# Where the prompt tiles, their norms and the retention scores stand in the order of an eight-core decoder step

## The reference: what is computed

```python
for layer in range(2):
    h = rms_norm(x, norm_mix[layer])
    if layer == 0:                       # retention, 4 heads, dk 256, dv 512
        q, k = rotate(h @ w_q), rotate(h @ w_k) / 16
        v = h @ w_v
        # per chunk of 128 tokens, state s (256 x 512) per head:
        #   o = (q k^T * decay) v + decay * q s ;  s = decay * s + k^T v
        o = group_norm(o)
        x = x + (silu(h @ w_g) * o) @ w_o
    else:                                # attention over a window of 128, sinks
        x = x + attention(h) @ w_o + b_o
    h = rms_norm(x, norm_ffn[layer])
    x = x + (silu(h @ w1) * (h @ w3)) @ w2
y = rms_norm(x, norm_final)
```

## Time and profile before

| what | value |
|---|---|
| median of 3 runs | 1962.94 us (1962.29 to 1965.96) |
| the profiled execution: its time | 1966.23 us |
| its span, on the slowest core | 1965.2 us (cores 1955.5 to 1965.2) |
| PE busy | 1852.6 us (94%) |
| DVE busy | 875.5 us (45%) |
| ACT busy | 677.4 us (34%) |
| mean granted clock of PE, slowest core | 0.986 |

### The profile page before, as it was taken

How to read it: one execution, slowest core, us unless ns; L and a number is a source line. 1 busy time by engine, 2 the same in 40 slices (tenths; PEclk the granted TensorE clock), 3 DMA queues, 4 the chain that set the end, 5 groups by cost and what they waited for, 6 DMA issues and landing times.

```text
span 1965.2 us, 29635 instructions; the slowest of 8 cores (1955.5 to 1965.2 us)
## 1 busy us (share of the span) xinstructions
PE 1852.6 (94%) x10167; PEld 853.7 (43%) x10167; DVE 875.5 (45%) x1549; ACT 677.4 (34%) x1062; POOL 222.0 (11%) x363
## 2 busy tenths in 40 slices
PE   4999999999999999999979998999999998999997
PEld 1444444344444334443434444445454543445453
DVE  3565543434346663433655554332222555522225
ACT  3544432321224742223344444221012366410112
POOL 0111111010101001110011111111011110011010
PEclk9899999999999999999989999999999999999999
DMA  9435565898987349998746655665335330254352
GB/s 194 68 66 87 94 81 87 199 207 197 210 203 144 46 84 220 217 202 228 160 108 113 106 94 84 119 82 74 54 57 78 56 58 9 33 88 69 54 71 97
DMA packets 216449, 220.79 MB, mean 112 GB/s; under 512 B 47824, under 2 KB 171088, under 8 KB 216272
## 3 DMA queue, kind: packets, MB, share of 16 engines
q0 software_dynamic: 128112, 114.08, 41.3%
q1 hardware_dynamic: 88192, 104.83, 17.9%
HBM read 277.10 MB, written 48.89 MB: 166 GB/s over the span
## 4 chain that ended last, share of the span: by engine, by line
PE 81%; DVE 7%; DMA 4%; issue 3%; ACT 3%; DVEq 0%; POOL 0%; SPq 0%; ACTq 0%; POOLq 0%
PE ps L579 81%; DVE rt L603 2%; DMA x_62<-xTp 1%; DMA uT_64<-g_73 1%; ACT sq L595 1%; DMA wr<-wa 1%; DVE h_44 L606 1%; DVE stat L858 1%; DMA x_63<-xTp 1%; DVE x_62 L606 0%; DVE h_45 L606 0%; DVE x_62 L603 0%; PE ps L584 0%; DMA yTp<-x_62 0%; ACT L593 0%
## 5 line engine op out<-in xcount | busy, mean ns | idle before, releaser
L579 PE MATMUL ps<-h_44,wr 128*128 128x512 bf16 x1824 | 411.3, 381 | 14.1 <-DMA wr<-wa 8.6
L579 PE MATMUL ps<-h_45,wr 128*128 128x512 bf16 x1824 | 413.1, 380 | 0.0
L579 PEld LDWEIGHTS ps<-h_44,wr 128*128 128x128 bf16 x1824 | 174.5, 98 | 230.4 <-issue 31.7
L579 PEld LDWEIGHTS ps<-h_45,wr 128*128 128x128 bf16 x1824 | 173.9, 98 | 217.1 <-issue 18.2
L259 POOL DMA_DIRECT2D wr<-w x152 | 112.9, 745 | 1017.0 <-PE ps L579 914.3
L579 PE MATMUL ps<-aT_105,wr 128*128 128x512 bf16 x704 | 157.7, 379 | 1.6 <-DVE x_62 L603 1.6
L579 PE MATMUL ps<-aT_103,wr 128*128 128x512 bf16 x704 | 157.0, 379 | 1.4 <-DVE aT_136 L603 1.4
L595 ACT ACTIVATE s_104<-ps 128x512 f32<-128x512 f32 x88 | 52.5, 596 | 305.5 <-PE ps L579 284.2
L603 DVE TENSOR_TENSOR aT_105<-s_106,ps 128x512 bf16<-128x512 f32 x88 | 60.5, 688 | 208.0 <-PE ps L579 179.0
L603 DVE TENSOR_TENSOR aT_103<-s_104,ps 128x512 bf16<-128x512 f32 x88 | 60.5, 688 | 204.2 <-PE ps L579 184.9
L579 PE MATMUL ps<-wr,h_44 128*128 128x512 bf16 (+1 forms) x576 | 130.5, 375 | 6.2 <-ACT rstd_57 L595 3.6
(11 more groups left out here) (288 smaller groups left out, 2147.2 us busy)
## 6 DMA issues: line engine op xcount, KB each, us to landing
wr<-w POOLq DMA_DIRECT2D x88, 512.0 KB, 7.5
wr<-wa POOLq DMA_DIRECT2D x24, 1024.0 KB, 12.4
wr<-w POOLq DMA_DIRECT2D x64, 352.0 KB, 7.0
wr<-wo POOLq DMA_DIRECT2D x16, 512.0 KB, 8.9
S_0_107<-st_in SPq DMA_DIRECT2D x16, 512.0 KB, 6.2
S_1_108<-st_in SPq DMA_DIRECT2D x16, 512.0 KB, 6.6
S_2_109<-st_in SPq DMA_DIRECT2D x16, 512.0 KB, 7.7
S_3_110<-st_in SPq DMA_DIRECT2D x16, 512.0 KB, 6.6
```

The costliest lines, as they stand in the source:

```text
L579: self.S.op("pe", lambda e: e.matmul(out, lhsT, rhs, start=start, stop=stop, skip_group_check=skip), r, w, dur=k * max(0.1, self.n(out) * ...
```

## The change

Four edits.

1. **The fourth x tile.** T[0]'s final norm writes into tiles of its own (`yo0`, `yo4`, `yo7`), placed over memory that `ffn` no longer uses. When it is done, T[3] is loaded by four DMAs on SP, and then y is stored by three DMAs on ACT's queue. In `ret_layer` the load of the spilled states (`Sin`) comes first, in memory of its own; then `pre()` completes T[0]'s norm before the other tiles of the layer are placed.
2. **Scores.** In `Rp` the scores of chunks 0 and 1 are written before the output of chunk 0, and those of chunk c + 2 after the state update of chunk c.
3. **Banks.** The norm of the second tile after `w_o` takes bank 6 or 7.
4. **The start.** The loads of T[1] are written before unit 2 (g of head 0) and start when unit 0 has landed; unit 2 waits for the third quarter of T[1]; unit 3 waits for nothing of x.

```diff
@@ norm_do_out
-            o, ob = (cx.x, cx.xb) if j.to_x else (cx.h, cx.hb)
-            self.stt(o[:, kc, :NT], cx.x[:, kc, :NT], self.gain(j.gi, kc), j.rstd_ap[:, :NT], ALU.mult, ALU.mult,
-                     [cx.xb[kc], j.rstd_buf, self.spb], [ob[kc]])
+            if callable(j.dst):
+                j.dst = j.dst()
+            if j.dst:
+                out, outb = j.dst[kc]
+            else:
+                o, outs = (cx.x, cx.xb) if j.to_x else (cx.h, cx.hb)
+                out, outb = o[:, kc, :NT], outs[kc]
+            self.stt(out, cx.x[:, kc, :NT], self.gain(j.gi, kc), j.rstd_ap[:, :NT], ALU.mult, ALU.mult,
+                     [cx.xb[kc], j.rstd_buf, self.spb], [outb])
@@ ret_layer
-        Ar = Area(M, self.a0, self.rid0)
+        Ar = Area(M, self.rid0 - 8192, self.rid0)
+        Sin = [Ar.tile(f"Sin{i}", [128, 2, 512], F32) for i in range(2)]
...
+        load_sin(0)
+        load_sin(1)
+        pre()
+        Ar = Area(M, self.a0, self.rid0 - 8192)
@@ Rp
                 if c == 0:
                     pcs.append(sc_piece(n))
+                    pcs.append(sc_piece(n + 1))
                 pcs.append((3, lambda n=n: r_o(n), need_o(n)))
                 pcs.append((2, lambda n=n: r_su(n), need_su(n)))
-                if c < 3:
-                    pcs.append(sc_piece(n + 1))
+                if c < 2:
+                    pcs.append(sc_piece(n + 2))
@@ program
         def rest():
-            load_x(1, 4, [self.ring.cur[("v", 0)][2]], True)
+            load_x(1, 4, [self.ring.cur[("qk", 0)][2]], True)
             load_rope(1)
-        self.ring.start({0: T[0].xb[4:6], 3: T[1].xb}, {3: rest})
+        self.ring.start({0: T[0].xb[4:6], 2: T[1].xb[4:6]}, {2: rest})
...
-                           [lambda: self.norm_begin(ta, 1, NBK), lambda: self.norm_begin(tb, 1, NBK), lambda: self.norm_begin(scx, 1, NBK)], s == 1)
+                           [lambda: self.norm_begin(ta, 1, NBK), lambda: self.norm_begin(tb, 1, (6, 7)), lambda: self.norm_begin(scx, 1, NBK)], s == 1,
+                           lambda: self.norm_now(T[0]) if s == 1 else None)
...
                 def endA():
+                    ys = []
+                    def place():
+                        for k, n, off in ((0, 4, 0), (4, 3, 8192), (7, 1, HF * TT * 4 + 8 * TT * 4)):
+                            t_, tb_ = M.tile(f"yo{k}", [128, n, TT], F32, self.a0 + off, n)
+                            ys.append((k, n, t_, tb_))
+                        return [(t_[:, i, :], tb_[i]) for k, n, t_, tb_ in ys for i in range(n)]
                     def aft():
-                        store(0)
-                        load_x(3)
-                    return self.norm_begin(ta, 4, NBK, True, aft)
+                        load_x(3, 4)
+                        for k, n, t_, tb_ in ys:
+                            self.dma("act", yout[:, k:k + n, 0:TT], t_[:, :, :], tb_, [], f"yo{k}")
+                    j = self.norm_begin(ta, 4, NBK, True, aft)
+                    j.dst = place
+                    return j
```

More of the change, by code:

```diff
@@ L666, in norm_begin @@
         j.cx, j.gi, j.pool, j.to_x, j.after = cx, gi, pool, to_x, after
-        j.sq, j.mm, j.nmm, j.out, j.bk, j.half = [], [], 0, None, None, None
+        j.sq, j.mm, j.nmm, j.out, j.bk, j.half, j.dst = [], [], 0, None, None, None, None
         self.jobs.append(j)
@@ L885, in dq_tick, with ret_layer, load_sin @@
                 self.force(it)
-    def ret_layer(self, s, cxs, scx, idle, first_norms, norms, wo_rider):
+    def ret_layer(self, s, cxs, scx, idle, first_norms, norms, wo_rider, pre):
         M = self.M
-        Ar = Area(M, self.a0, self.rid0)
+        Ar = Area(M, self.rid0 - 8192, self.rid0)
+        Sin = [Ar.tile(f"Sin{i}", [128, 2, 512], F32) for i in range(2)]
+        def load_sin(h):
+            if s == 1 and h < RH:
+                self.dma("sp", Sin[h % 2][0][:, :, :], self.DR["spill"][h].rearrange("(a p) e -> p a e", p=128),
+                         [self.spillb[h]], Sin[h % 2][1], f"sin{h % 2}")
+        load_sin(0)
+        load_sin(1)
+        pre()
+        Ar = Area(M, self.a0, self.rid0 - 8192)
         uT0 = Ar.tile("uT0", [128, 16, TT], BF16, 16)
@@ L906, in ret_layer @@
         Sbf = [Ar.tile(f"Sbf{i}", [128, 2, 512], BF16) for i in range(2)]
-        Sin = [Ar.tile(f"Sin{i}", [128, 2, 512], F32) for i in range(2)]
         cf, cfb, cb, cbb = self.cf, self.cfb, self.cb, self.cbb
@@ L917, in ret_layer @@
                             g=Rr.tile(f"rg{h}", [128, 512], BF16))
[L919 to L924, removed]
         def P(h, ti, lead=False):
```

## The result

The changed kernel took 1950.88 us (median of 4 runs, 1949.41 to 1955.07), the kernel before 1964.45 us on the same chip (4 runs, 1962.29 to 1969.34): a ratio of 0.9931, 95% interval 0.9905 to 0.9957, 13.6 us faster. In a second comparison it took 1951.34 us, ratio 0.9923 (0.9905 to 0.9941). Forecast: 15.4 us faster, 1948.

A forecast was written before the change was run, and what follows sets the result against it. PE was taken as the bound, busy 1852.6 of 1965.2 us. Terms of -6.0, -9.5, -3.0 and +3.1 gave -15.4 us, from the median 1962.94 to 1947.5, stated as 1948; range 1938 to 1960.

The forecast's parts named there:

- The likeliest case: Whole kernel: 15.4 us faster, to 1948 us, with a range of 10 to 20 us faster; chance 0.47.
- 1, fourth tile: End of round 0: T[3] lands earlier through parallel loads, so the group at its norm starts sooner; 6.0 us gained.
- 2, scores: Retention outputs: masks written one chunk earlier remove PE's waits for `sT`; 9.5 us gained of 11.7 at most.
- 3, banks: Third group of `ffn` in each round: no more wait for the bank of the second tile's norm; 3.0 us gained.
- 4, start: Start: g lands later and PE stands for it, less a part regained by the clock; costs 3.1 us.
- a gain by the clock: Start: the group after the second g group runs at the high clock, 1.89 instead of 3.57 us; 1.7 us gained.
- a fifth was kept back: Score waits: four fifths of 11.7 us counted, 9.5, since the state's copy `Sbf` might end as late as the mask.
- The third rival: Score matmuls: PE stands for the first mask before the second score at all 16 pairs; 8.5 us slower, 1971; chance 0.08.
- the prediction's own +4.8: Start: the second g group begins at 55.7 instead of 50.92 us because g lands later; 4.8 us lost.
- The first rival: Start: g of head 0 lands at 43.3, before PE asks at 44.6; 22 us faster in all, 1941; chance 0.12.
- that I counted as none: Around T[3]'s norm: 2.7 us lost to low clock might return, but none was counted since 2 us of standing remain.
- the stand at the group that I feared for: PE's 0.84 us wait at 977.66 for T[1]'s norm, feared longer behind ACT's store issues; 1 us charged.

The follow-up runs named there:

- undo2: The changed kernel with the score reordering taken back; 1964.37 us, ratio 1.0002 to the kernel before.
- undo4: The changed kernel with the reordered start loads taken back; 1942.70 us, ratio 0.9900 to the kernel before; 1944.92 us, 0.9897 when repeated.
- only4: The kernel before with only the reordered start loads added; 1971.75 us, ratio 1.0028 to the kernel before.
- g_free: The changed kernel with T[1] still loaded early, but g of head 0 issued directly behind v, not held for T[1]; 1951.84 us, ratio 0.9921 to the kernel before.
- split: The changed kernel with only T[1]'s first two quarters loaded early, the last two after v, and g not held; 1946.29 us, ratio 0.9900 to the kernel before.
- undo1: The changed kernel with the fourth-tile change taken back: y in place, T[3] loaded by two serial halves; 1954.86 us, ratio 0.9951 to the kernel before.
- store_sp: The changed kernel with y's three stores on SP's queue behind the loads instead of on ACT's; 1953.34 us, ratio 0.9924 to the kernel before.
- undo3: The changed kernel with the use of banks 6 and 7 taken back; 1954.66 us, ratio 0.9956 to the kernel before.
- undo4_first67: The changed kernel without the reordered start loads, first norms of T[1] and T[3] also in banks 6 and 7; 1956.40 us, ratio 0.9946 to the kernel before.

## Why the prediction came out

The likeliest case held: faster by 13.6 us where 15.4 was said, inside the likeliest one's own range of 10 to 20. Term by term, each against its edit taken back (in us; the last four columns are means over cores, from one execution each; edit 4 also from its repeat):

| edit | predicted | by the ratios | mean span | standing | 0.16 x stands | clock |
|---|---|---|---|---|---|---|
| 1, fourth tile | -6.0 | -4 | -4.1 | -1.6 | +0.3 | -1.9 |
| 2, scores | -9.5 | -14 | -15.6 | -9.5 | -2.7 | -3.1 |
| 3, banks | -3.0 | -5 | -2.9 | -2.9 | -0.6 | +1.2 |
| 4, start | +3.1 | +6 | +5.4 | +5.3 | +0.2 | +1.1 |
| 4, repeated | +3.1 | +5 | +5.9 | +5.4 | +0.3 | +0.5 |

The four mean spans add up to -17.2, and the mean span fell by 17.7. The waits were found at the right places. What was off is their price: edit 2 was priced by the idle time of the listed waits alone, edit 1 on one core, and edit 4 with a gain by the clock that didn't come.

**Edit 2** is the term that was furthest off, and the mechanism held. All 11.7 us of `sT` went; 1.9 us for `Sbf` and some for `uT` came (a fifth was kept back for this). The third rival, a stand in front of the second score, didn't occur: no score matmul waits. From the first score matmul of a round to the first matmul of w2, both rounds together, undo2 takes 727.2 us and the changed kernel 713.3: 13.9 us, not 9.5. The list of waits leaves out gaps of 0.15 us and less: of the 64 matmuls on `sT`, 23 or 24 stand in undo2, 12.7 us in the mean over cores, not 13 with 11.7, and none in the changed kernel. Each stand costs 0.16 us on top, 3.8 us for these matmuls. The clock of the table needs care: 2.3 of its 3.1 us lie after 1300 us, behind the last matmul on `sT` (1220.8), and are not shown to be of this edit.

**Edit 4**. The mechanism held step by step: T[1]'s third quarter at 38.0 (36.7 predicted), g issued at 38.6 (37), landed at 50.5 (49.4), 11.9 us (12.4; 10.3 to 14.6 over the cores), second g group at 56.6 (55.7). From the first projection to the first score matmul the changed kernel takes 36.7 us in the mean over cores, undo4 31.9, and the repeats 37.5 and 32.7: 4.8 us both times, the prediction's own +4.8 without its clock. The step that failed is "the next group then runs at the high clock, 1.89 instead of 3.57 us: -1.7". Around the two stands the clock was low for 6.8 to 10.2 us on the eight cores, in the kernel before for 3.4 to 6.8 us, and on core 0 the second group ran at 3.45 us too. Part of this low time fell on standing, where it costs nothing; what PE lost while it worked was 0.8 and 1.2 us more at the start than without edit 4 (3.6 and 2.8; 3.8 and 2.6), and only4 lost as much as the kernel before (3.3 and 3.4). So nothing was given back. g_free and split show where the standing is from: part from holding g back until T[1] has landed (3.1 of 4.6 us of standing, 2.1 of 4.8 us of the stretch), the rest from T[1] sharing the DMA engines with v and g. The first rival, g in time, had no core for it: PE stood 3.8 to 8.2 us for g on all eight.

The Trainium skill, "DMA: Bandwidth & Descriptors", section "Anatomy of one DMA — SWDGE (gpsimd) path", gave an estimate of 6.8 us for g; the trace has 10.3 at the least, so the rows were the better guide.

**Edit 1**: the sum was right for the core it was read on. T[3] landed 15.2 us after its issue (986.68 - 971.47; 13 predicted) and the group at its norm came 9.8 us after PE was through with T[2]'s values (994.50 - 984.68; 9.3 predicted, 996.2 - 986.93). Of the wait of 4.42 us 2.49 remain, and the 11.9 us from the row sum to that group became 7.3 (994.50 - 987.17), as said, though not all by the cause that was said. PE's stand for the eviction of g, 1.53 us, is gone: ACT's squares run in one go, where those of the second half had come late and g behind them. But another 1.6 us are the clock: the first group of g took 3.51 us before and takes 1.89 now. And core 3 was the one whose tile came last. There the group came 16.3 us after T[2]'s values; on the other seven cores it was 13.1 to 14.6 before, and after it is 9.8 to 11.1 on all eight. The wait itself was 2.49 to 2.97 us on these seven already before, and after it is 2.49 or 2.50 on all eight. These 2.49 us are ACT's queue: its squares of T[3] begin at 985.25, behind the last `v` eviction, though the first quarter landed at 979.75.

From the end of T[2]'s values to T[3]'s first projection undo1 takes 19.4 us in the mean over cores and the changed kernel 14.7 (14.9 in its repeat): 4.7 us, of which 2.4 is standing (1.8 of it between the row sum and the group, 0.4 at the row sum) and most of the rest the clock, 0.97 or more in place of 0.90 to 0.93, that I counted as none. I charged 1 us for ACT's store issues; the stand at the group that I feared for is 0.86 us against 0.84, now for DVE's rotation, and store_sp shows that the queue doesn't matter.

The rule of the Trainium skill that transfers of all queues share the engines ("DMA: Bandwidth & Descriptors", "Issuing engines are not separate DMA queues") agrees: T[3] came in with y, 986.68 and 985.39. On this core it cost PE nothing, because ACT came to the squares no sooner.

**Edit 3**: 2.9 us of standing for 3.0, but the equality is luck. The two stands of 1.53 us are back in undo3 on all cores. Other waits before 1300 us are 2.2 us shorter there (those for `uT` 1.6), and after 1300 us it stands 2.0 us longer (1.9 of it for DVE's `aT`), where the prediction had nothing. Why was not tested.

That the sum was near is in part luck: edit 2 gave 4 us more than said, edit 4 cost 2 more and edit 1 gave 1 to 2 less.

## What to carry to other kernels

A load that is put ahead of another delays it twice, by the bytes in between and by the wait that orders them; compare when each is asked for first (T[1]'s squares here had to wait for ACT's `v` evictions anyway). Before pricing a wait at one core's number, read it on all cores: 4.42 us on the slowest, 2.49 to 2.97 on the others. Price a stand by when the next matmul starts, not by its idle time: here each cost 0.16 us more, and ten of 23 were too short for the list. Don't count on the clock to give something back behind a stand: here it gave nothing.

## What was not expected of the hardware

The clock: of two stands with a group of 8 matmuls between them, cores showed one low stretch or two behind the same program. In the changed kernel the low level lasted 6.8 us at the start on some cores and 10.2 on others, with stands of the same order (5.71 and 1.75 us on core 2, 5.62 and 1.26 on core 3). Single cores are therefore no measure of an edit of this size. The mean over eight is a better one: the mean span of the changed kernel was 1942.4 and 1942.9 us, that of undo4 1937.0 both times, and the clock 16.6 and 15.8, 15.5 and 15.3. An edit's clock of 1 us is within that spread.

In ten of the thirteen executions a granted clock of 0.81 showed as well, for 0.9 to 15.1 us at a time and on two neighbouring cores together (6.3 us from 37 us on cores 4 and 5 of undo4, begun ahead of both stands). It cost up to 2.0 us in the mean over cores and did not follow the edits: the changed kernel had none in one execution and 0.5 us in the next.

Freeing a bank made a kernel slower (undo4_first67): the `rstd` waits fell from 4.8 to 2.0 us in the mean over cores, while the standing rose by 2.7 us, the stands by 17 and the clock by 3.9 us.
